# An expert's U and V rows fetched in one gather, and dot products handed on in pairs

## What is computed

```python
def peer(h, w_q, sub_keys, u_tab, v_tab):
    ...
        gate = jax.nn.softmax(best.astype(jnp.float32), axis=-1).astype(xc.dtype)
        u = jnp.take(u_tab, e, axis=0)
        hid = jax.nn.gelu(jnp.einsum('cd,chkd->chk', xc, u), approximate=False)
        vsel = jnp.take(v_tab, e, axis=0)
        return jnp.einsum('chk,chkd->cd', gate * hid, vsel)
```

## Time and profile before

| | us |
|---|---|
| median of 3 runs (lowest, highest) | 9257.01 (9247.52, 9277.42) |
| profiled execution, span | 9253.9 |
| the first layer's `stage_retrieve`, first gather to last addition | 1895.2 |
| the second layer's | 1912.5 |
| busy over the span: PE, DVE, POOL, ACT | 7315.0, 4618.2, 3234.3, 1801.1 |

### The profile page before, as it was taken

One profiled execution on the slowest core, in us unless ns is written; L12 is line 12 of the kernel. 1 busy time (PEld: TensorE's weight loads), 2 busy tenths in 40 slices (PEclk: granted clock), 3 DMA queues, 4 the chain that ended last, 5 costly groups with the idle time before them and its releaser, 6 DMA issues. The chain is left out here.

```text
span 9253.9 us, 95340 instructions
## 1 busy us (share of the span) xinstructions
PE 7315.0 (79%) x31078; PEld 4507.4 (49%) x31078; DVE 4618.2 (50%) x10131; ACT 1801.1 (19%) x3910; POOL 3234.3 (35%) x3073
## 2 busy tenths in 40 slices
PE   6888888889867676776678888889898677666766
PEld 2777776745433222222237777777454322222322
DVE  1555544550375555555525554555304755555555
ACT  1232222210111111111112222221101111111111
POOL 0001001100027777777601100101000377777775
PEclk8999998999988888888889999999998888888888
DMA  3000000112139999999830000001111499999997
GB/s 136 16 9 9 9 9 10 30 35 60 42 107 372 349 366 352 350 363 347 317 131 9 9 9 9 13 14 30 39 52 49 171 367 349 347 357 346 368 336 283
DMA packets 627068, 1521.21 MB, mean 164 GB/s; under 512 B 56546, under 2 KB 285560, under 8 KB 626808
## 3 DMA queue, kind: packets, MB, share of 16 engines
q0 software_dynamic: 368640, 1342.34, 39.0%
q1 hardware_dynamic: 257600, 174.74, 6.2%
q10 hardware_dynamic: 568, 0.22, 0.0%
HBM read 1513.43 MB, written 3.67 MB: 164 GB/s over the span
## 5 line engine op out<-in xcount | busy, mean ns | idle before, releaser
L1793 PE MATMUL ps<-arena 128*128 128x512 f32 x5120 | 2622.3, 671 | 1118.9 <-ACT arena L1686 1116.8
L1793 PEld LDWEIGHTS ps<-arena 128*128 128x128 f32 x5120 | 1075.0, 215 | 2667.7 <-ACT arena L1686 1356.4
L1732 DVE CUSTOM_DVE_ANT_0 arena<-arena 128x1024 f32<-128x1024 f32 x1280 | 1555.5, 1227 | 1314.6 <-DMA arena<-peer_u,arena 1295.0
L424 PE MATMUL ps<-h,w 128*128 128x512 f32 x5056 | 1474.9, 452 | 310.0 <-issue 131.1
L1667 POOL DMA_INDIRECT arena<-peer_v,arena x1280 | 1437.9, 1123 | 417.9 <-issue 339.7
L1667 POOL DMA_INDIRECT arena<-peer_u,arena x1280 | 1373.8, 1073 | 514.6 <-issue 329.3
L424 PEld LDWEIGHTS ps<-h,w 128*128 128x128 f32 x5056 | 811.9, 199 | 966.4 <-issue 903.1
L690 POOL MEMSET arena<- 64x640 f32 (+1 forms) x80 | 44.7, 559 | 1853.0 <-POOLq L83 1849.4
L1764 ACT ACTIVATE arena<-arena 128x4 f32<-128x4 f32 x320 | 66.1, 207 | 2949.1 <-DVEq L1737 2949.1
L966 DVE TENSOR_TENSOR arena<-ps,level 128x512 f32<-128x512 f32 (+1 forms) x480 | 273.3, 601 | 478.6 <-PE ps L757 476.2
L763 PE MATMUL ps<-arena 128*128 128x128 f32 x3200 | 409.4, 285 | 51.9 <-DVE arena L966 51.9
(11 more groups left out here) (288 smaller groups left out, 8761.6 us busy)
## 6 DMA issues: line engine op xcount, KB each, us to landing
w<-w_in SPq DMA_DIRECT2D x132, 512.0 KB, 4.0
arena<-ada_w SPq DMA_DIRECT2D x24, 2048.0 KB, 12.2
arena<-peer_u,arena POOLq DMA_INDIRECT x1280, 6.1
arena<-peer_v,arena POOLq DMA_INDIRECT x1280, 6.2
w<-peer_wq SPq DMA_DIRECT2D x32, 512.0 KB, 6.6
w<-w_a_out SPq DMA_DIRECT2D x16, 512.0 KB, 3.6
w<-w_out SPq DMA_DIRECT2D x16, 512.0 KB, 3.8
w<-w_b_out SPq DMA_DIRECT2D x16, 256.0 KB, 2.6
```

The lines of the kernel that those rows point to most:

```text
L424: mm = eng.matmul(psum[:, c0:c0 + n], m.w[:, slot, k, :], src[:, k, c0:c0 + n], start=(k == 0), stop=(k == KB - 1))
L1732: eng.tensor_tensor_reduce(ub[:, r, :], ub[:, r, :], hs, 1.0, 0.0, ALU.mult, ALU.add, hid[:, i:i + 1]).then_inc(u_free, 1)
L1793: mm = eng.matmul(m.bank(j), dg[:, r, :], vb[:, r, 512 * j:512 * j + 512], start=False, stop=False)
```

## The change

The host lays U and V side by side in one table `peer_uv`, 8 KB a row. One gather per slot brings both into one buffer `uv` of a ring of 8, so the ring holds as many bytes as the two rings before. The buffer is free (`freed`) when TensorE's matmul of the slot is done, the dot product no longer frees anything. The lead of U over V is gone, since both come at once. `SUB` is 2 instead of 4, so `hid_done`, Gelu, weights and diagonals go by pairs; the four parts of the selection stand at every fourth pair, which is every eighth slot, as before.

```diff
-    SUB = 4
+    SUB = 2
     QS = GROUP // SUB
-    LEAD = 4
...
-    ub, vb, dg = m.take(RING, D), m.take(RING, D), m.take(RING, P)
+    uv, dg = m.take(RING, 2 * D), m.take(RING, P)
...
-    ut = d["peer_u"].rearrange("l e c -> (l e) c")
-    vt = d["peer_v"].rearrange("l e c -> (l e) c")
+    table = d["peer_uv"].rearrange("l e c -> (l e) c")
...
-    def gather(eng, g, i, free, table, buf, landed):
-        off = bass.IndirectOffsetOnAxis(ap=stage.bitcast(U32)[:, i % GROUP:i % GROUP + 1], axis=0)
-        eng.wait_ge(free, g * GROUP + (i + 1))
+    def gather(eng, g, i):
+        if i % HALF == 0:
+            stage_rows(eng, g, i // HALF)
+        off = bass.IndirectOffsetOnAxis(ap=stage.bitcast(U32)[:, i:i + 1], axis=0)
+        eng.wait_ge(freed, g * GROUP + (i + 1))
         eng.sem_inc(asked, 1)
-        eng.indirect_dma_start(buf[:, i % RING, :], None, table, off).then_inc(landed[i % RING], 16)
...
+        eng.indirect_dma_start(uv[:, i % RING, :], None, table, off).then_inc(uv_in[i % RING], 16)
...
         @block.gpsimd
         def _(eng):
-            stage_rows(eng, 0, 0)
-            for i in range(LEAD):
-                gather_u(eng, 0, i)
-            with eng.Fori(0, TILES * GROUPS_T - 1) as g:
+            with eng.Fori(0, TILES * GROUPS_T) as g:
                 for i in range(GROUP):
...
+                    gather(eng, g, i)
...
-                        eng.tensor_tensor_reduce(ub[:, r, :], ub[:, r, :], hs, 1.0, 0.0, ALU.mult, ALU.add,
-                                                 hid[:, i:i + 1]).then_inc(u_free, 1)
+                        eng.wait_ge(uv_in[r], before + g * (16 * (GROUP // RING)) + 16 * (i // RING + 1))
+                        eng.tensor_tensor_reduce(uv[:, r, 0:D], uv[:, r, 0:D], hs, 1.0, 0.0, ALU.mult, ALU.add,
+                                                 hid[:, i:i + 1]).then_inc(summed_u, 1)
...
-                            if q % 2 == 0:
-                                select_part(ch, w, g + GROUPS_T, q // 2, shifted, exped, g + 1)
+                            if q % 4 == 0:
+                                select_part(ch, w, g + GROUPS_T, q // 4, shifted, exped, g + 1)
...
-                            mm = eng.matmul(m.bank(j), dg[:, r, :], vb[:, r, 512 * j:512 * j + 512], start=False, stop=False)
-                        mm.then_inc(v_free, 1)
+                            mm = eng.matmul(m.bank(j), dg[:, r, :], uv[:, r, D + 512 * j:D + 512 * j + 512], start=False, stop=False)
+                        mm.then_inc(freed, 1)
...
+    inputs["peer_uv"] = np.concatenate([inputs.pop("peer_u"), inputs.pop("peer_v")], axis=2)
```

More of the change, by code:

```diff
@@ L116, in __init__ @@
         self.used = 0
-        self.u_in = [ctx.enter_context(nc.semaphore(f"u_landed{i}")) for i in range(RING)]
-        self.v_in = [ctx.enter_context(nc.semaphore(f"v_landed{i}")) for i in range(RING)]
+        self.uv_in = [ctx.enter_context(nc.semaphore(f"uv_landed{i}")) for i in range(RING)]
         self.qkv_in = [ctx.enter_context(nc.semaphore(f"rwkv_weights{i}")) for i in range(3)]
@@ L1631, in stage_retrieve @@
     s = st.sem
-    SUB = 4
+    SUB = 2
     QS = GROUP // SUB
-    LEAD = 4
     HALF = GROUP // 2
-    u_in, v_in = m.u_in, m.v_in
+    uv_in = m.uv_in
     before = l * (16 * TILES * SLOTS // RING)
-    u_free, v_free, hid_done, gel_done, w_done, dg_done, staged, g_in = (
-        s(n) for n in ("u_free", "v_free", "hid_done", "gelu_done", "weights_done", "diag_done", "staged", "gates_in"))
+    summed_u, freed, hid_done, gel_done, w_done, dg_done, staged, g_in = (
+        s(n) for n in ("u_summed", "freed", "hid_done", "gelu_done", "weights_done", "diag_done", "staged", "gates_in"))
     dve, pair, shifted, exped, selected = (s(n) for n in ("dve", "pair", "shifted", "exponentials", "selected"))
@@ L1661, in stage_rows @@
         eng.wait_ge(staged, g * 2 + (half + 1))
-    def gather(eng, g, i, free, table, buf, landed):
-        off = bass.IndirectOffsetOnAxis(ap=stage.bitcast(U32)[:, i % GROUP:i % GROUP + 1], axis=0)
-        eng.wait_ge(free, g * GROUP + (i + 1))
-        eng.sem_inc(asked, 1)
-        eng.indirect_dma_start(buf[:, i % RING, :], None, table, off).then_inc(landed[i % RING], 16)
[L1669 to L1673, removed]
+    def gather(eng, g, i):
[3 more added lines that the diff above has]
+        eng.wait_ge(freed, g * GROUP + (i + 1))
+        eng.sem_inc(asked, 1)
+        eng.indirect_dma_start(uv[:, i % RING, :], None, table, off).then_inc(uv_in[i % RING], 16)
     def weights(eng, g, q):
@@ L1684, in diag @@
         for i in range(SUB * q, SUB * q + SUB):
-            eng.wait_ge(v_free, g * GROUP + (i + 1))
+            eng.wait_ge(freed, g * GROUP + (i + 1))
             eng.activation(dg[:, i % RING, :], m.ident[:, :], ACT.Copy, scale=wgt[:, i:i + 1]).then_inc(dg_done, 1)
@@ L1712, in _ @@
             eng.sem_inc(selected, GROUPS_T)
-            eng.sem_inc(u_free, RING)
             eng.sem_inc(x_out, 1)
@@ L1730, in _ @@
                         r = i % RING
-                        eng.wait_ge(u_in[r], before + g * (16 * (GROUP // RING)) + 16 * (i // RING + 1))
-                        eng.tensor_tensor_reduce(ub[:, r, :], ub[:, r, :], hs, 1.0, 0.0, ALU.mult, ALU.add,
-                                                 hid[:, i:i + 1]).then_inc(u_free, 1)
+                        eng.wait_ge(uv_in[r], before + g * (16 * (GROUP // RING)) + 16 * (i // RING + 1))
+                        eng.tensor_tensor_reduce(uv[:, r, 0:D], uv[:, r, 0:D], hs, 1.0, 0.0, ALU.mult, ALU.add,
+                                                 hid[:, i:i + 1]).then_inc(summed_u, 1)
                         if i % SUB == SUB - 1:
                             q = i // SUB
-                            eng.wait_ge(u_free, g * GROUP + (RING + i + 1))
+                            eng.wait_ge(summed_u, g * GROUP + (i + 1))
                             eng.sem_inc(hid_done, 1)
@@ L1766, in _ @@
                             diag(eng, g, q - 1)
-                        if q == 4:
+                        if q == 8:
                             eng.wait_ge(shifted, g + 1)
@@ L1780, in _ @@
             eng.wait_ge(zeroed, 1)
-            eng.sem_inc(v_free, RING)
+            eng.sem_inc(freed, RING)
             with eng.Fori(0, TILES) as t:
@@ L1789, in _ @@
                         r = i % RING
-                        eng.wait_ge(v_in[r], before + g * (16 * (GROUP // RING)) + 16 * (i // RING + 1))
+                        eng.wait_ge(uv_in[r], before + g * (16 * (GROUP // RING)) + 16 * (i // RING + 1))
                         eng.wait_ge(dg_done, g * GROUP + (i + 1))
                         for j in range(2):
-                            mm = eng.matmul(m.bank(j), dg[:, r, :], vb[:, r, 512 * j:512 * j + 512], start=False, stop=False)
-                        mm.then_inc(v_free, 1)
+                            mm = eng.matmul(m.bank(j), dg[:, r, :], uv[:, r, D + 512 * j:D + 512 * j + 512], start=False, stop=False)
+                        mm.then_inc(freed, 1)
                 for i in range(2):
```

## The result

| | before | after |
|---|---|---|
| median of the runs side by side, us | 9263.26 (9247.52 to 9277.42, 4 runs) | 9129.23 (9121.36 to 9142.38, 4 runs) |
| span of the profiled execution, us | 9253.9 | 9135.3 |
| granted clock, mean over the span | 0.894 | 0.911 |
| stage, first layer / second layer, us | 1895.2 / 1912.5 | 1847.4 / 1843.9 |

The ratio is 0.9857, 95% interval 0.9841 to 0.9872: 1.4% faster, where 4% was forecast, and 4 us above the top of the range. The two stages give 47.8 + 68.6 = 116.4 of the span's 118.6 us, so the change acted where it was expected to, but with a third of the expected 371 us. Here are the page's GB/s row and the gathers' queue, which answer to the earlier trace rows.

What follows compares the result with a forecast made beforehand. GpSimd's gathers were taken as the bound, transfers as next: a layer sums to 5.7 + 1633.9 + 62.4 + 16.3 = 1718.3 us, two layers save 371.1, span 8882.8, plus 3.1 gives about 8885 us; range 8790 to 9125.

Steps and rivals of the forecast that it cites:

- The bound before: Inside a tile GpSimd issues gathers end to end and sets the time: two gathers with pauses, 2.79 us a slot.
- The rival of a bound memory: Random rows give only the mean 358 GB/s: 2.93 us a slot, 9361 us in all; chance 0.05.
- The price of the new gather: On GpSimd, one 8 KB-row gather costs the old one's 1.09 us plus 0.30 pause: 1.4 us a slot.
- What the transfers can do: The 16 DMA engines with never-empty queues: 410 GB/s, 2.557 us a slot; 2.486 if a row is one packet.
- The ring: Eight buffers: holding plus refill takes 17.5 us and fits into 8 x 2.557 = 20.5, with 3.0 to spare.
- what is late next: the transfers: Once GpSimd leaves the path, DMA transfers set the time inside a tile at 2.557 us a slot.
- Part 0: Where this selection part (3.9 us) intervenes, the pair ahead waits 13.3 us; with refill 19.0, leaving 1.5 to spare.
- Pairs hidden under the transfers: Pairs add 160 multiplications on VectorE and 160 Gelu calls on ScalarE a layer, some 60 us, covered by transfers.
- The change of a tile: Between tiles the first refill lands at T + 38.6 instead of T + 23.0: 15.6 us each, four a layer.
- The stalls stay: Part of the packets' time is the memory's: up to 2.74 us a slot, 9120 us in all; chance 0.16.
- TensorE's lower clock: Between pairs TensorE falls to 1.2 GHz: 2.94 us a slot, 9375 us; chance 0.10 shared with a ring run dry.
- a ring run dry: The eight buffers fail to keep transfers fed; chance 0.10 shared with TensorE's lower clock.

Runs made afterwards that it cites:

- before_no_hold: The kernel before, two gathers kept, without dot products, Gelu, weights and diagonals; TensorE multiplies V by the identity: 8811.48 us (one run).
- sub1: The changed kernel with dot products handed on one by one instead of in pairs: 8769.91 us, ratio 0.9486 to the kernel before.
- no_hold: The changed kernel without dot products, Gelu, weights and diagonals; TensorE multiplies each V half by the identity once landed: 8652.22 us (one run).
- sub1_lag2: sub1 with weights and diagonals one dot product later, so every slot waits two dot products: 8891.25 us, ratio 0.9606 to the kernel before.
- sub1_lag3: sub1 with weights and diagonals two dot products later, so every slot waits three dot products: 9229.42 us, ratio 0.9976 to the kernel before.
- sub4: The changed kernel with dot products handed on in fours instead of pairs: 11871.08 us (one run).

## Why the prediction was half right

**The bound before: right.** GpSimd set the time, and not the memory: its waits for nothing have shrunk from 331.1 to 82.5 us, and `before_no_hold` is 4.8% shorter by its span (8809.7) with the same transfers. The rival of a bound memory falls with 422 GB/s held over 1560 us, and with 410 for rows of 4 KB. The Trainium skill's page "DMA: Bandwidth & Descriptors" (Specifications) gives about 358 GB/s as one core's share of the memory, which spoke for that rival. With 410 and 422 this one core went above it, so the figure did not limit it.

**The price of the new gather: right.** It was taken as the old one's 1.093 us, and is 1.125.

**What the transfers can do: right as a capacity.** 2.557 us a slot was taken, with a bound below of 2.486 for one packet a row. That bound is what came: `sub1` and `no_hold` run at 2.485 inside a tile.

**The ring: this step failed**, and with it "what is late next: the transfers". It found that 17.5 us of holding and refilling fit into 8 x 2.557 = 20.5, with 3.0 to spare, and took the queues as never empty from that. A round of eight slots takes 8 x 2.77 = 22.2 us in fact. Of these 8.7 are the median from issue to landing, where the step had 5.7 from a lone gather, and the 13.4 that are left are holding and issuing again, where it had 3 x 2.557 + 1.3 + 1.0 + 1.8 = 11.8. Of the 1.6 in between, 0.6 are only the three slots' own slower pace, and the step has no term for the time from a matmul's end to the refill's issue. (13.4 goes over both slots of a pair, 11.8 is for the first alone, which takes 13.8 on average in the trace.) The larger error is the refill.

The step treated slack as yes or no: if the mean fits, the queues are full. But the engines go round in jerks. Part 0 was seen to leave 1.5 us to spare, and it does more than that: TensorE idles, buffers come free in a bunch, and their refills stand in line while the queues had run low just before.

At part 0 the holding was mis-sized too. In the timeline above, the first slot of the pair ahead of part 0 has landed at 2987.98, where its dot product starts, and the next gather into its buffer is the one at 3004.52: 16.5 us, where the step had 13.3. Most of the difference stands behind TensorE's pause: from the start of the matmuls at 2999.93 that gather is 4.6 us away, where the step had 1.8. In the burst that began at 2986.08 after 0.29 us of idling, the same way took 2.8 us (to the gather at 2988.88). So about 1.0 us is the missing term, and 1.8 us goes with a slow start (granted clock 0.79 between 3000 and 3010). The step names up to 2.3 us for a burst that starts slow, but does not add them at part 0, though the slow burst of the earlier trace rows is the one behind part 0. With them 19.0 + 2.3 = 21.3 would not have fitted into 20.5.

What a ring needs is the holding plus a refill time *in line*. The singles have it: a round of 8 x 2.485 = 19.9 less a landing of 11.4 leaves 8.5 for holding, so transfers always queue and the rate is 422. The same subtraction gives 10.8 us of holding at 404 GB/s (`sub1_lag2`), 13.4 at 378 (the changed kernel) and 14.4 at 370 (`sub1_lag3`).

The slot's time alone makes the difference. 639 slots at 2.77 instead of 2.557 are 136 us more a layer; the stages are 1847.4 - 1718.3 = 129 and 1843.9 - 1718.3 = 126 above the forecast. With 2.485 the same sum gives 84.4 + 1587.9 = 1672 us, and the stages of `sub1` take 1665, from first gather to last addition.

**Pairs hidden under the transfers: right for VectorE's and ScalarE's work, wrong as a choice.** `sub1` has twice as many of these steps and is the faster. That fours would have been worse is shown by `sub4`, but pairs still held the buffers too long for a full rate.

**The change of a tile: right**, 14.3 us against 15.6.

**The rivals.** "The stalls stay" named 9120 us, close to the 9129 that were measured, for a wrong reason: it put 2.74 us a slot down to the memory. TensorE's lower clock did not decide as that rival had it, between all pairs: the granted clock in the long stretches is 0.90 and 0.91, where it was 0.86, and `sub1` has its 422 GB/s at 0.94. Low means (1.00 is 2.4 GHz, 0.50 is 1.2 GHz) stand above where TensorE had idled long, as the 0.67 behind 13.21 us and the 0.79 behind 6.71. What those slow starts alone cost, no run separates. The other half of that rival, a ring run dry, is what happened, with a tenth of a chance and priced only as TensorE's pace.

## What to carry to other kernels

When two buffers that come free at different times are joined, the joined one is held as long as the longer, and the ring must be checked anew. Holding plus the refill time in line, not that of a lone transfer, must fit into the ring's slots. A slack of a seventh, worked out from means, is none when one engine stops for four microseconds now and then. Hand on in the smallest step first, and read issue-to-landing times together with the rate: a long landing at a full rate is a healthy queue, and a landing near its minimum at a low rate is a starved one.

## What was not expected of the hardware

- One core held 422 GB/s of random rows of 8 KB for 1560 us, with one packet per row; with rows of 4 KB in two gathers it was 410 over 270 us.
- GpSimd's cost for a gather of 128 rows depends on what VectorE does beside it, not on the row: 0.946 us for 4 KB and 0.948 for 8 KB rows with VectorE quiet, 1.093 for 4 KB and 1.125 for 8 KB rows beside dot products (means over a stage or more).
